# Encoder layer with experts: the order of the eight halves of the out-projection

## What is computed

```
merged = g_a * (attention_a @ w_branch_a) + g_b * (attention_b @ w_branch_b)   # gates g_a, g_b
x1     = layer_norm(ALPHA * x + merged @ w_out, ln1_g, ln1_b)                  # 512 x 1024 a sequence
y      = sum over 16 experts of gate[e] * ((silu(a) * u) @ w_eo[e]),  a, u = split(x1 @ w_ei[e])
out    = layer_norm(ALPHA * x1 + y, ln2_g, ln2_b)
```

## Time and profile before

| | |
|---|---|
| median of three runs | 1375.24 us |
| lowest, highest | 1374.85, 1378.96 us |
| the profiled execution, time | 1373.68 us |
| its span | 1372.0 us |
| TensorE busy | 1263.2 us (92%) |
| VectorE busy | 709.0 us (52%) |
| ScalarE busy | 633.2 us (46%) |
| GpSimd busy | 354.6 us (26%) |
| chain that ended last | TensorE 78%, VectorE 9%, issue 5% |

### The profile page before, as it was taken

One profiled execution on the slowest core, in us unless ns is written; L12 is line 12 of the kernel. 1 busy time (PEld: TensorE's weight loads), 2 busy tenths in 40 slices (PEclk: granted clock), 3 DMA queues, 4 the chain that ended last, 5 costly groups with the idle time before them and its releaser, 6 DMA issues.

```text
span 1372.0 us, 19228 instructions
## 1 busy us (share of the span) xinstructions
PE 1263.2 (92%) x7198; PEld 1035.3 (75%) x7199; DVE 709.0 (52%) x896; ACT 633.2 (46%) x856; POOL 354.6 (26%) x295
## 2 busy tenths in 40 slices
PE   5999899999989999899999989599999999999970
PEld 4888767788869888866788867477788888778860
DVE  4233367321656333366321565767746575874556
ACT  4232466422323222477422322567645565774445
POOL 0532000000210332000000110248734655874330
PEclk9999999999999999999999999599999999999995
DMA  6832200033353332200024362469977987996326
GB/s 214 266 127 93 92 1 2 3 107 136 113 224 133 104 102 93 93 1 2 1 92 141 105 245 107 157 227 310 348 226 213 307 270 244 320 342 224 95 48 246
DMA packets 65339, 211.74 MB, mean 154 GB/s; under 512 B 14359, under 2 KB 14871, under 8 KB 64471
## 3 DMA queue, kind: packets, MB, share of 16 engines
q1 hardware_dynamic: 50492, 178.32, 37.5%
q0 software_dynamic: 12192, 24.00, 7.1%
q10 hardware_dynamic: 2592, 8.53, 1.6%
HBM read 200.13 MB, written 34.25 MB: 171 GB/s over the span
## 4 chain that ended last, share of the span: by engine, by line
PE 78%; DVE 9%; issue 5%; ACT 4%; POOL 2%; DMA 2%; ACTq 0%; SPq 0%; DVEq 0%; POOLq 0%
PE banks L701 21%; PE banks L702 20%; PE banks L703 20%; PE banks L867 2%; PE banks L831 2%; PE banks L902 2%; DVE moe_lo L1403 2%; PE banks L909 2%; PE banks L983 1%; POOL gated L601 1%; PE banks L842 1%; DMA moe_raw<-in_expert_w 1%; PE banks L735 1%; PE banks L1008 1%; DVE wlo L1422 1%
## 5 line engine op out<-in xcount | busy, mean ns | idle before, releaser
L1249 ACT ACTIVATE moe_hi<-moe_raw 128x2048 fp32r<-128x2048 f32 x102 | 195.1, 1917 | 51.0 <-PE banks L703 30.6
L1422 DVE TENSOR_TENSOR wlo<-raw,whi 128x2048 fp32r<-128x2048 f32 (+1 forms) x52 | 116.0, 2231 | 184.6 <-ACT whi L1092 184.6
L1403 DVE TENSOR_TENSOR moe_lo<-moe_raw,moe_hi 128x2048 fp32r<-128x2048 f32 x86 | 195.1, 2289 | 22.0 <-ACT moe_hi L1249 21.8
L701 PE MATMUL banks<-xT,whi 128*128 128x512 f32 x448 | 175.5, 392 | 0.0
L702 PE MATMUL banks<-xT,whi 128*128 128x512 f32 x448 | 174.9, 390 | 0.0
L703 PE MATMUL banks<-xT,wlo 128*128 128x512 f32 x448 | 174.8, 390 | 0.0
L701 PE MATMUL banks<-wlo,xT 128*128 128x256 f32 (+1 forms) x448 | 136.8, 305 | 18.5 <-DVE wlo L1422 18.5
L601 POOL TENSOR_TENSOR gated<-gated,kqv 128x512 f32<-128x512 f32 x16 | 25.3, 1598 | 496.6 <-DVE kqv L1564 496.6
L701 PE MATMUL banks<-moe_lo,xeh 128*128 128x512 f32 x368 | 146.4, 398 | 5.4 <-DVE moe_lo L1403 3.8
L703 PE MATMUL banks<-moe_hi,xel 128*128 128x512 f32 x368 | 144.9, 394 | 0.0
L702 PE MATMUL banks<-moe_hi,xeh 128*128 128x512 f32 x368 | 144.9, 394 | 0.0
(11 more groups left out here) (262 smaller groups left out, 2334.9 us busy)
## 6 DMA issues: line engine op xcount, KB each, us to landing
moe_raw<-in_expert_w SPq DMA_DIRECT2D x192, 512.0 KB, 5.7
raw<-in_front_w SPq DMA_DIRECT2D x104, 512.0 KB, 4.5
toeplitz_rows<-bias_rows POOLq DMA_DIRECT2D x4, 1152.0 KB, 14.1
kqv<-in_x_turned SPq DMA_DIRECT2D x8, 512.0 KB, 7.8
pt<-in_x SPq DMA_DIRECT2D x2, 2048.0 KB, 9.9
x_rows<-pt ACTq DMA_DIRECT2D x8, 512.0 KB, 2.7
token_sums<-pt ACTq DMA_DIRECT2D x8, 512.0 KB, 3.7
sum_tile<-token_sums SPq DMA_DIRECT2D x8, 512.0 KB, 6.4
```

Of the source, the lines that this page charges most:

```text
L701: mm(dst, left[0], right[1], start=first, stop=False)
L1249: A(moe_hi[m % SPLIT_E], moe_raw[m % RAW_E], ACT.Copy).then_inc(e_hi, 1)
L1403: V.tensor_tensor(moe_lo[m % SPLIT_E], moe_raw[m % RAW_E], moe_hi[m % SPLIT_E].bitcast(F32), ALU.subtract).then_inc(lo_sem(m % ECH), 1)
L1422: V.tensor_tensor(view(lo, shape), view(raw[c % 2], shape), view(hi, shape).bitcast(F32), ALU.subtract).then_inc(w_split, 1)
```

## The change

The eight products are issued in the order (0,0), (1,0), (0,1), (1,1), and then as before. A list `OUT_ORDER` carries this order, and product numbers, PSUM banks and `out_done` follow from the place in the list. VectorE takes the residuals in the same order. Its `finish(0)` no longer stands behind the residual of (1,0), but directly behind the variance of tile 0, that is behind (0,1) and ahead of (1,1). From tile 2 on nothing moves.

```
+OUT_ORDER = [(0, 0), (1, 0), (0, 1), (1, 1)] + [(_t, _h) for _t in range(2, TT) for _h in range(N_OUT_MM)]
 LAST_OUT = MM_OUT + N_OUT_MM * (TT - 1)
 def out_done(t):
-    return MM_OUT + N_OUT_MM * (t + 1)
+    return MM_OUT + OUT_ORDER.index((t, 1)) + 1
...
# TensorE
-                    n = MM_OUT + N_OUT_MM * t + h
+                    n = MM_OUT + OUT_ORDER.index((t, h))
...
-                for t in range(TT):
-                    for h in range(N_OUT_MM):
-                        out_half(h, t)
+                for t, h in OUT_ORDER:
+                    out_half(h, t)
+                    if h == 0:
+                        continue
                     if t >= 1:
                         turn_x1(s, t - 1)
...
# VectorE
-                for t in range(TT):
-                    for h in range(N_OUT_MM):
...
+                for t, h in OUT_ORDER:
+                    col = slice(h * 512, (h + 1) * 512)
+                    n = MM_OUT + OUT_ORDER.index((t, h))
+                    b = mm_wait(n)
+                    V.scalar_tensor_tensor(xr[:, t, col], xr[:, t, col], ALPHA, b[:, :], ALU.mult, ALU.add) \
+                        .then_inc(residual, 1)
+                    dve.wait_ge(residual, s * TT * N_OUT_MM + n - MM_OUT + 1 + 4)
+                    o = (t * N_OUT_MM + h) * 6
+                    ins = V.bn_stats(stats[:, o:o + 6], xr[:, t, col])
+                    if h == 0 and t >= 2:
+                        finish(t - 1)
...
+                    if h == 1:
+                        chain(ins)
+                        chain(V.bn_aggr(mv[:, 2 * t:2 * t + 2], stats[:, t * N_OUT_MM * 6:(t + 1) * N_OUT_MM * 6]))
+                        V.tensor_scalar(rstd1[:, t:t + 1], mv[:, 2 * t + 1:2 * t + 2], LN_EPS, None, ALU.add).then_inc(ln_var, 1)
+                        if t == 0:
+                            finish(0)
```

More of the change, by code:

```diff
@@ new lines, in _ @@
+                for t, h in OUT_ORDER:
[9 more added lines that the diff above has]
+                        finish(t - 1)
+                    if s + 1 < SEQS and h == 0 and t == 3:
+                        split_lo(0, s + 1)
+                    if s + 1 < SEQS and h == 0 and t == 2:
+                        x_lo(s + 1, 0)
+                    if h == 0 and t == 3:
+                        logit(s, 0)
+                    if h == 1:
[4 more added lines that the diff above has]
+                            finish(0)
```

## The result

| | before | changed |
|---|---|---|
| median, first comparison (8 and 8 runs) | 1375.55 us | 1367.73 us |
| second comparison (16 and 6 runs) | 1375.41 us | 1367.82 us |
| third comparison (11 and 6 runs) | 1375.29 us | 1366.51 us |
| span of the first profile | 1372.0 us | 1366.5 us |

The ratio is 0.9947 (95% interval 0.9932 to 0.9962) in the first comparison, 0.9945 (0.9929 to 0.9960) in the second and 0.9943 (0.9923 to 0.9964) in the third. The kernel became 7.6 to 8.8 us faster; 1366.5 with a range of 1363 to 1371 had been forecast. In the changed file the lines of TensorE's helper are one further on (L702 to L704 for L701 to L703), VectorE's split is L1424, its `merge_lo` L1550.

The account below looks back on a forecast made before the run. TensorE, busy for 92% of the span, was taken to bound the kernel. 5.28 us for the gaps plus 3.44 for the clock, 8.72 in all, off a median of 1375.24 gave 1366.5 us, range 1363 to 1371.

Parts of the forecast that it names:

- The gap: TensorE's wait for the second weight chunks between (0,0) and (0,1) in the out-projection: vanishes, 2.64 us a sequence, 5.28 together.
- The clock behind it: TensorE's slow stretches at 1.2 GHz behind the out-projection's wait: both go, 3.44 us taken, bounds 0 and 3.44.
- Rival A: Out-projection: the wait goes but the short waits in (0,0) keep the lower clock; 1369.96 us, chance 0.20.
- `finish(0)`: VectorE's epilogue of tile 0, moved: ready 0.33 us before TensorE asks at `turn_x1(0)`, cost taken as 0.
- Rival B: A new TensorE wait at `turn_x1(0)`, as root or residual come late; at 1 us a sequence 1368.5 us, chance 0.07.
- VectorE, SyncE, the norm's parameters: Out-projection: VectorE's first residuals, SyncE's loads and the parameters `finish(0)` needs all come in time; cost 0.
- The earlier start carries to the end: Stages behind the out-projection hang on TensorE, VectorE or each other, none on absolute time, so the whole 8.72 us lead stays.
- Rivals C and D: Experts' loop: C, a load wait swallows the lead, about 1375 us, chance 0.09; D, extra load waits, slower, 0.04.
- D's price: Experts' loop: chain waits for a load, 6.63 and 5.95 us, come once more each; with both 1379.1 us, chance 0.04.
- The sum: Whole kernel: 5.28 us from the out-projection's waits plus 3.44 us from the clock, 8.72 us gained.

Follow-up runs that it names:

- the filler: Kernel before, old order, with ten extra 128x512 matmuls into an unused PSUM bank right behind (0,0): 1370.16 us, ratio 0.9969 to before.
- late `finish(0)`: Changed kernel with `finish(0)` behind the variance of tile 1 instead of tile 0: 1381.07 us, ratio 1.0044 to the kernel before.

## Why the prediction was right

- *The gap*: 2.64 us a sequence, forecast to vanish whole. It did, 2.87 to 0.22 between two starts.
- *The clock behind it*: the upper end, 3.44 us, was taken over the bound 0. In the pair of profiles it came true, and the filler shows the mechanism. That it came in both sequences of the one profile that was read was luck: over five profiles the low stretch came in 6 of 10 gaps, so 2.1 us on the average. The timed runs of before spend more at the lower clock than these profiles, an estimated 2.9 us worth beyond the changed kernel, so the profiles' 2.1 may be too low for a typical run; how much of it stands behind the gaps no run shows.
- *Rival A*, with the rule of the Trainium skill on short idle moments ("TensorE: Matmul & The Clock Gate", "A second HAM failure mode: psum-queue depth-cycling"): the short waits stayed and the clock held in twelve of twelve stretches, and again with the filler. No run here bears the rule out for waits of 0.6 to 0.8 us.
- *`finish(0)`*: margin 0.33 us, measured 0.33. Rival B did not come. The late `finish(0)` shows that the place which it named is the critical one: one place later costs 4.65 us a sequence.
- *VectorE, SyncE, the norm's parameters*: nobody waited, as costed.
- *"The earlier start carries to the end"*: this step failed by 2.2 us. The lead carries whole into the loop and shrinks there. Rivals C and D had looked at the loop, and the argument against them was that all its partners shift together. They don't: the loop starts 8.77 us earlier, its first load only 4.0 (805.28 before, 801.25 now), since that load hangs on the splits of the second sequence, which carry the lead of the first alone. That this makes the loop longer is not shown; with the late `finish(0)` the loads had more time ahead of the loop (807.71 to 905.4) and it was as long. D's price was also misread: 6.63 and 5.95 us are the stretches of the chain that belong to a load, not waits. In that profile TensorE's longest wait for an expert's weights was 2.3 us and ScalarE's longest wait for a load 2.1:

```profile
PE banks L701 <- DVE moe_lo L1403: 3.8, 2, 2.3
...
ACT moe_hi L1249 <- DMA moe_raw<-in_expert_w: 18.1, 19, 2.1
```

- *The sum*: 8.72 us against a measured 7.6 to 8.8. It is right within the intervals (5.2 to 9.4 in the first comparison). Part of the agreement is luck: a loss of 2.2 us in the loop was not in the sum, and the timed runs of before lost more to the clock than its profiles. With the profiles' values it would be 5.2 us, which is the lower edge of the intervals; the mean clocks of the timed runs account for most of the way from there to the measured gain, by an estimate and not by a run made for it.

## What to carry to other kernels

Where an engine waits for a second set of operands, look for work behind it that needs only the first set, and count the matmuls against the wait: 24 against a gap of 12 here. Then move the epilogue along with it, and add up the chain from the last product to whoever asks next; here the epilogue was ready 0.33 us before it was wanted, and one place later made the kernel slower than before. A short gap on TensorE can cost its clock too; filling it with useless matmuls is a quick experiment that tells the two costs apart. A few profiles can be quicker than the typical run: compare their mean clock with that of the timed runs before adding up from them.

## What the hardware showed that was not expected

- A gap of 2.9 us between two matmuls of the same code lowered TensorE's clock to 1.2 GHz for 3.4 us in 6 of 10 cases. A wait of 4.65 us lowered it for 3.4 us in one sequence and for 6.8 in the other.
- The experts' loop, the same instructions in the same order, got 2.2 us (0.5%) longer with an exchange of two products in the stage ahead of it, whether it started earlier or later than before. In experts that have two blocks of 128 rows of tokens to work on, the first silu and the second lie 12.25 us apart in every profile; all of the scatter lies in the experts with one block.
- The mean clock tells slow executions of one kernel from quick ones that are otherwise alike: in 27 runs of the kernel before it lies between 0.961 and 0.968, and the ten runs with 0.961 or 0.962 average 1377.4 us, the fifteen with 0.966 to 0.968 average 1373.5.
